# Rotated keys of odd cached pages, and a second copy of the rotated queries, on partitions 64 to 127

## The reference

```
def key_inv_rms(rows, w_uk):
    kn = einsum('...kl,lhd->...khd', rf[..., :KV_LORA], w_uk)
    ss = sum(kn * kn, -1) + sum(rf[..., KV_LORA:] ** 2, -1)[..., None]
    return rsqrt(ss / QK_DIM + EPS)

s = (einsum('...qhl,...kl->...hqk', q_lat, rows[..., :KV_LORA])
     + einsum('...qhd,...kd->...hqk', q_eff[..., NOPE_DIM:], rows[..., KV_LORA:]))
s = s * r
p = softmax(where(mask, s, -inf))
o_lat = einsum('...hqk,...kl->...qhl', p, rows[..., :KV_LORA])
```

## Time and profile before

| what | value |
|---|---|
| median of 3 runs | 2373.68 us (2371.53 to 2374.73) |
| the profiled execution, its own time | 2373.9 us |
| its span, first to last instruction | 2372.1 us |
| mean granted TensorE clock | 0.972 |
| TensorE busy | 2228.7 us, 94% of the span |
| VectorE, ScalarE, GpSimd busy | 1348.9, 1112.7, 1077.8 us |
| sample attention stage | 1440 to 2217 us |

### The profile page before, as it was taken

One profiled execution on the slowest core, in us unless ns is written; L12 is line 12 of the kernel. 1 busy time (PEld: TensorE's weight loads), 2 busy tenths in 40 slices (PEclk: granted clock), 3 DMA queues, 4 the chain that ended last, 5 costly groups with the idle time before them and its releaser, 6 DMA issues. The chain is left out here.

```text
span 2372.1 us, 39390 instructions
## 1 busy us (share of the span) xinstructions
PE 2228.7 (94%) x13958; PEld 1903.2 (80%) x13958; DVE 1348.9 (57%) x2187; ACT 1112.7 (47%) x2840; POOL 1077.8 (45%) x712
## 2 busy tenths in 40 slices
PE   6999999999999998799999986999999999999689
PEld 5989898989888987589997764777777777777489
DVE  4766676767676767552126656565555565655410
ACT  4455545454545454543344534554444444545222
POOL 5565656565555655156760005433333333333065
PEclk8999999999999999799999987999999999999899
DMA  4564646464646464234442312212202112022444
GB/s 155 200 222 162 230 167 219 171 216 169 226 163 228 168 217 160 99 128 158 152 151 108 111 57 79 66 31 61 70 22 71 33 52 68 25 66 61 191 151 138
DMA packets 80349, 309.83 MB, mean 131 GB/s; under 512 B 14578, under 2 KB 21874, under 8 KB 54690
## 3 DMA queue, kind: packets, MB, share of 16 engines
q1 hardware_dynamic: 80162, 307.38, 38.5%
HBM read 279.56 MB, written 27.79 MB: 130 GB/s over the span
## 5 line engine op out<-in xcount | busy, mean ns | idle before, releaser
L671 POOL TENSOR_TENSOR w_lo<-raw,w_hi 128x1024 fp32r<-128x1024 f32 x218 | 540.8, 2501 | 363.0 <-ACT w_hi L861 362.9
L122 PE MATMUL bank<-h_hi,w_hi 128*128 128x304 f32 x1776 | 552.3, 311 | 25.4 <-POOLq L254 13.5
L124 PE MATMUL bank<-h_hi,w_lo 128*128 128x304 f32 x1776 | 538.3, 303 | 0.0
L123 PE MATMUL bank<-h_lo,w_hi 128*128 128x304 f32 x1776 | 536.1, 302 | 0.0
L122 PE MATMUL bank<-b_hi,a_hi 128*128 128x512 f32 x896 | 363.3, 406 | 26.8 <-issue 15.0
L861 ACT ACTIVATE w_hi<-raw 128x1024 fp32r<-128x1024 f32 x216 | 216.6, 1050 | 350.3 <-PE bank L124 350.3
L122 PEld LDWEIGHTS bank<-h_hi,w_hi 128*128 128x128 f32 x1776 | 335.8, 189 | 41.2 <-POOLq L254 13.7
L123 PE MATMUL bank<-b_lo,a_hi 128*128 128x512 f32 x896 | 356.5, 398 | 0.0
L124 PE MATMUL bank<-b_hi,a_lo 128*128 128x512 f32 x896 | 356.0, 397 | 0.0
L123 PEld LDWEIGHTS bank<-h_lo,w_hi 128*128 128x128 f32 x1776 | 337.0, 190 | 2.3 <-issue 1.7
L124 PEld LDWEIGHTS bank<-h_hi,w_lo 128*128 128x128 f32 x1776 | 336.2, 189 | 0.0
(11 more groups left out here) (368 smaller groups left out, 3943.1 us busy)
## 6 DMA issues: line engine op xcount, KB each, us to landing
raw<-in_a_units SPq DMA_DIRECT2D x112, 1024.0 KB, 5.0
raw<-in_b_in_units SPq DMA_DIRECT2D x20, 1024.0 KB, 4.9
past<-in_cache SPq DMA_DIRECT2D x64, 288.0 KB, 3.3
s_in<-in_state_in SPq DMA_DIRECT2D x32, 512.0 KB, 6.9
s_t<-in_state_t SPq DMA_DIRECT2D x16, 1024.0 KB, 6.3
out_state_out<-s_in SPq DMA_DIRECT2D x32, 512.0 KB, 6.8
pt<-in_cache_t SPq DMA_DIRECT2D x64, 256.0 KB, 2.6
raw<-in_o_units SPq DMA_DIRECT2D x16, 1024.0 KB, 5.1
```

What stands on the lines that cost most here:

```text
L122: nc.tensor.matmul(out, a[0], b[0], start=start, stop=False)
L123: nc.tensor.matmul(out, a[0], b[1], start=False, stop=False)
L124: return nc.tensor.matmul(out, a[1], b[0], start=False, stop=stop)
L671: nc.gpsimd.tensor_tensor(w_lo[u % 2][:, c], raw[u % 2][:, c], w_hi[u % 2][:, c].bitcast(F32), ALU.subtract).then_inc(lo_done, 1)
```

## The change

The tile `pk` gets 128 partitions; the rotated part of an even page is loaded into partitions 0 to 63 and that of an odd page into 64 to 127. The tile `q_rss` gets 128 partitions and is written twice per sequence, once in each half. In `scores` the odd page's rotated product reads both operands from partitions 64 to 127. The product with the new tokens' keys reads the lower half. The bytes per partition of both tiles and their addresses stay as they are.

```
-                                  ("q_ls", [P, LT, QROWS]), ("q_rss", [ROPE, QROWS]), ("smx", [QROWS, 2]), ...
+                                  ("q_ls", [P, LT, QROWS]), ("q_rss", [P, QROWS]), ("smx", [QROWS, 2]), ...
...
-    ... (("pt", [P, LATENT]), ("pk", [ROPE, P]))]
+    ... (("pt", [P, LATENT]), ("pk", [P, P]))]
...
+def rope_rows(k):
+
+    return slice(k % 2 * ROPE, (k % 2 + 1) * ROPE)
...
-    sp.dma_start(m[f"pk{u}"][:], d["cache_rt"][bass.ds(page, 1)].rearrange("a p n -> (a p) n")).then_inc(turned_in[u], 16)
+    sp.dma_start(m[f"pk{u}"][rope_rows(k), :], d["cache_rt"][bass.ds(page, 1)].rearrange("a p n -> (a p) n")).then_inc(turned_in[u], 16)
...
                 for e in range(2):
-                    nc.tensor.matmul(SA[u][e * QROWS:(e + 1) * QROWS, cols], m["q_rss"][:], pk[(k + e) % TURNED][:], start=False, stop=True).then_inc(s_done.sem, 1)
+                    r = rope_rows(e)
+                    nc.tensor.matmul(SA[u][e * QROWS:(e + 1) * QROWS, cols], m["q_rss"][r, :], pk[(k + e) % TURNED][r, :], start=False, stop=True).then_inc(s_done.sem, 1)
...
-                nc.tensor.matmul(dst, m["q_rss"][:], m["kr_s"][:], start=False, stop=True).then_inc(new_done.sem, 1)
+                nc.tensor.matmul(dst, m["q_rss"][0:ROPE, :], m["kr_s"][:], start=False, stop=True).then_inc(new_done.sem, 1)
...
-                nc.vector.tensor_copy(m["q_rss"][:], m["q_rs"][:, bass.ds(s, 1), :].rearrange("p a q -> p (a q)")).then_inc(q_staged.sem, 1)
+                nc.vector.tensor_copy(m["q_rss"][0:ROPE, :], m["q_rs"][:, bass.ds(s, 1), :].rearrange("p a q -> p (a q)"))
+                nc.vector.tensor_copy(m["q_rss"][ROPE:P, :], m["q_rs"][:, bass.ds(s, 1), :].rearrange("p a q -> p (a q)")).then_inc(q_staged.sem, 1)
```

More of the change, by code:

```diff
@@ L1282, in memory_mla @@
     region(0, big + 8 * TOK * 4, [("past", [P, PAGES, ROW]), ("sc0", [QROWS, PAGES * P + N_SAMPLE]), ("sc1", [QROWS, PAGES * P + N_SAMPLE]),
-                                  ("q_ls", [P, LT, QROWS]), ("q_rss", [ROPE, QROWS]), ("smx", [QROWS, 2]), ("smx2", [P, 1]), ("ss1", [P, PAGES, MLA_HEADS])])
+                                  ("q_ls", [P, LT, QROWS]), ("q_rss", [P, QROWS]), ("smx", [QROWS, 2]), ("smx2", [P, 1]), ("ss1", [P, PAGES, MLA_HEADS])])
     region(big + 8 * TOK * 4 + 512, 2 * big, [("q_lat", [P, LT, DEC_BATCH, QROWS])])
@@ L1290, in memory_mla @@
     ring_at = 3 * big
-    region(ring_at, ring_at + 6 * UNIT * 4, [(f"{n}{k}", shape) for k in range(TURNED) for n, shape in (("pt", [P, LATENT]), ("pk", [ROPE, P]))]
+    region(ring_at, ring_at + 6 * UNIT * 4, [(f"{n}{k}", shape) for k in range(TURNED) for n, shape in (("pt", [P, LATENT]), ("pk", [P, P]))]
            + [(f"a_{x}{n}", [P, 256], F32R) for n in range(7) for x in ("hi", "lo")] + right[5, 1] + right[6, 0] + right[6, 1])
```

## The result

The changed kernel takes 2378.64 us in the median of 10 runs (2375.84 to 2382.26), the kernel before 2373.68 in 10 runs beside it (2370.62 to 2375.7). The ratio is 1.0022, with a 95% interval of 1.0013 to 1.0030: slower by 5.0 us, between 3.1 and 7.1. The forecast was 2375.8 us in a range of 2372.0 to 2381.5, so the sign and the wide range hold. The size is more than twice what I had summed, and the time lies 0.2 us beyond the range of 2373.5 to 2378.4 us that I gave the case I believed in, the one with the copies alone. By the 4.7 us that I took as what can be told from no change, 5.0 lies just on the slower side, which had a chance of 0.18.

The account below looks back on a forecast made before the run. TensorE, busy 742.45 of 777 us in the sample attention, was taken as the bound. TensorE 0, queue 0 and copies +2.1 us on 2373.7 gave 2375.8 us (+0.09%), range 2372.0 to 2381.5.

Parts of the forecast that it names:

- the case I believed in: Extra copies on VectorE cost time, TensorE's work unchanged: 2375.8 us, own range 2373.5 to 2378.4, chance 0.66.
- the slower side: Measurably slower than before, beyond about 4.7 us: chance 0.18, from row tiles taking turns (0.13) and mostly the clock (0.05).
- TensorE's part, 0: Rotated products in the sample attention: no matmul added, the two tiles already overlap, so other rows change nothing: 0 us.
- The rival in which the row tiles take turns: Rotated products on different rows writing one PSUM bank run one after the other: +7.0 us, 2382.8; chance 0.13.
- the one in which switches vanish: Tiles on disjoint rows spare 0.24 us per rotated group: 7.7 us gained, 2368.1 us; chance 0.04.
- The queue's part, 0: Page loads on the DMA queue: same packets to other partitions, some 15 us of cover before TensorE's products: 0 us.
- The way of the copy: At a sequence's start the copy delays VectorE's first addition, then ScalarE's squares and r, and so TensorE's wait.
- The two prices: New VectorE copy per sequence: +0.21 us if ahead of GpSimd's first sum, +0.65 or +0.75 if GpSimd is first.
- a term that I had put in without a row: Sequence 0: the copy stands ahead of the first subtraction on which TensorE waits: +0.1 us.
- The sum, 2.1: Copies over eight sequences: 0.65 + 0.75 + 3 x 0.21 + 0.1 = 2.1 us, bounds 1.2 to 4.7.
- the clock: Rival: TensorE's clock falls after the longer waits for r; two falls cost 3.3 us, 2379.1; chance 0.07.
- The hidden copy in sequence 3: Sequence 3, after a loop turn: the addition idles 0.36 us for TensorE, which hides the new copy: 0 us.

Follow-up runs that it names:

- the first trace: Profiled execution of the changed kernel as described, its fastest run: 2375.84 us.
- the three traces: Three profiled executions of the same changed kernel, nothing further altered: 2375.84, 2380.09 and 2377.12 us.
- The second trace of before: The kernel before, unchanged, run once more for a second profile: 2372.37 us.

## Why the forecast was right, and where its size was off

**TensorE's part, 0.** Right. The group kept its 0.43 and 0.37 us, and the change without the second copy has the time of before within 0.09%. The rival in which the row tiles take turns is out, and the one in which switches vanish is out by the same rows. The Trainium skill, TensorEngine Tiling (Array Packing), Restrictions and Gotchas, says that different row tiles cannot use one PSUM bank at the same time. The trace doesn't agree with it as it is worded: two row tiles that write different partitions of one bank need no more time than two tiles on the same rows. The measurement decides. Two row tiles into the same partitions of a bank stand in no run here.

**The queue's part, 0.** Right, by the same experiment.

**The way of the copy.** Right at each step: no idle time ahead of the addition, squares behind it, r behind them, TensorE at r. Four experiments show it: added alone it costs as much as the change, moved 1.5 us down it is free, doubled it costs 8.6 us, and with r ahead of the squares it costs nothing where it stands but the 0.3 us of sequence 0.

**The price per copy.** The two prices hold: 0.2 us where the copy is first (gap 1.84 to 2.04 in sequence 2), 0.65 to 0.79 where GpSimd is first (gap of sequence 7, 1.76 to 2.49). In sequence 0 the copy cost 0.3 instead of 0.1, a term that I had put in without a row: the first subtraction starts 0.41 us after the old copy (1439.29 to 1439.70), and it was 0.10 before.

```profile
1439.29 0.18 DVE L2560 COPY q_rss<-q_rs 64x64 f32<-64x64 f32 x1
1439.48 0.19 DVE L2561 COPY q_rss<-q_rs 64x64 f32<-64x64 f32 x1
1439.70 2.90 DVE L2533 TENSOR_TENSOR b_lo<-uk_stage,b_hi 128x1024 fp32r<-128x1024 f32 x2
```

**The sum, 2.1: the step that was mis-sized.** I worked out from one trace who is first in each sequence, as if it were fixed. It isn't: in the first trace GpSimd won sequences 4 and 7, not 2 and 7, and that it won two in that trace, as forecast, is luck. The mean came near all the same: the wait for r grew by 3.3, 3.1 and 1.5 us in the three traces (12.5, 12.3 and 10.7 against 9.2), 2.6 on average, where I had 2.0. What I left out of the sum, as a rival with a chance of 0.07, was the clock, and it is a part of the ordinary case. I had its price right, about 1.6 us a fall. The three traces hold 0, 2 and 1 falls behind a wait for r, and the first one lacks a fall that the kernel before has behind a loop turn.

From the first copy of q_rss to the last wait for r the three take 2.1, 6.6 and 3.4 us more than the trace of before. The terms add up to that within 0.2: 3.2 + 0.3 - 1.6 = 1.9, 3.1 + 0.3 + 2 x 1.6 = 6.6 and 1.5 + 0.3 + 1.6 = 3.4 (gaps, sequence 0, falls). The second trace of before takes 0.8 us more than the first there, so much is scatter. On average that is 4.0 of the 5.0 us, 2.6 from the waits, 0.3 from sequence 0 and 1.0 from the clock, inside the interval of 3.1 to 7.1. Whether the remaining 1.0 is more of the same in the executions without a trace stays open. That the measured time lies inside the stated range is in part luck: of what reaches from 2378.4 us, the end of the copies' own range, to 2381.5, only the clock's 2379.1 had a sum behind it.

**The hidden copy in sequence 3.** In the first trace of the changed kernel the gap there rose from 1.5 to 2.6 us, where I had put 0. Behind the loop turn the clock stayed high (0.56 before), TensorE was sooner at its next product, and the addition no longer waited for it but started straight behind the copies:

```profile
1737.30:1741.10 3.80, 3.76 (x16) 3.10 (x17) 2.25 (x4) 1.19 (x3) 0.08 (x1) 1.00 0.34 92
...
1742.57 0.68 DVE L2561 COPY q_rss<-q_rs 64x64 f32 x1
1743.28 1.29 DVE L2576 TENSOR_TENSOR two<-bank,one 128x512 f32<-128x512 f32 x2
```

The kernel with the copy behind the additions shows how much of this is the copy's. In sequence 5 of its trace the clock stayed high too, only the old copy stood ahead of the additions, and the gap was 2.35:

```profile
1936.09 0.72 DVE L2560 COPY q_rss<-q_rs 64x64 f32 x1
1936.82 1.29 DVE L2575 TENSOR_TENSOR two<-bank,one 128x512 f32<-128x512 f32 x2
...
1941.76 0.60 PE L2479 MATMUL bank<-ident,r 128*64 128x128 f32 x4 [1.97 <-ACT r L2361]
```

Sequences 3 and 5 have the same gap before, 1.5. So 0.9 of the 1.1 us comes with the clock that stayed high, and about 0.3 is left for the new copy. TensorE had gained 1.6 us by the fall that didn't come, which is a part of why this execution is the fastest of the ten and its span is only 1.9 us longer. One span beside another would have given too small a cost.

## What to carry to other kernels

Price a small instruction by what stands behind it on its engine, not by its duration: a copy that takes 0.19 us by itself cost 5 us, because the addition behind it led to the one wait of the bounding engine, and it cost nothing that could be measured 1.5 us further down. When an addition to a kernel lengthens a wait, look whether the waited-for result has to come that late at all: here it stood behind eight squares that did not need it, and moving it gained twice what the change had lost. And what depends on which of two engines starts first by some hundredths of a microsecond should be given as a share of sequences, not read from one trace.

## What the runs showed of the hardware

A VectorE copy of 64x64 waits for a GpSimd instruction that began 0.05 us earlier, to its end (0.73 us instead of 0.19), while a VectorE reduction of the same size at the same place takes 212 to 214 ns each time, one that began 0.03 us after such an instruction among them. Two matmuls on different row halves and different column halves of the array, both into one PSUM bank, run at the pace of two on the same rows (269/294/320 ns, 0.43 us for four records, in every trace). And a pause of TensorE can cost more than its length: after 5 of 16 waits of 1.9 to 2.9 us the granted clock fell to the lower level, which cost 1.6 us each time; after the 54 waits of up to 1.8 us that I followed it did not.
